# Attention stages of a two-block transformer kernel: row maxima two units ahead, gate passes ahead of the value product

## The chip, the core and the metric

The kernel runs on one core of one Trainium2 chip. The metric is device time in microseconds (us) of one execution. TensorE (PE in the profile; its weight loads are the row PEld) multiplies into PSUM, the banks named `ps`; VectorE is DVE, ScalarE is ACT, GpSimd is POOL, SyncE is SP and issues the DMAs. Each engine has its own instruction stream and works through it in the order written; a stream waits for another engine by semaphores.

## The reference, cut to what matters

Two transformer blocks, each of two layers, work on one sequence of 512 tokens with 1024 channels. The softmax attentions below make up the stages that the change touches. Everything else (projections, convolution, feed-forward) stays as it is.

```python
# first block, per layer: 8 MLA heads (q, k of 96), then 8 heads with two branches each
s = jnp.einsum('bqhd,bkhd->bhqk', qb, k) * scale
p = masked_softmax(s, pos[None, :] <= t[:, None])
o = jnp.einsum('bhqk,bkhd->bqhd', p.astype(dt), v)      # MLA
...
p_s = masked_softmax(s_s, m_s); o_s = einsum(p_s, v_sel)  # selected blocks (at 512 tokens: all blocks)
p_w = masked_softmax(s_w, m_w); o_w = einsum(p_w, v_w)    # window
...
# second block, per layer: 8 sparse heads (a mask of the top 128 keys), 8 forgetting heads
p = jax.nn.softmax(logits, axis=-1); out = jnp.einsum("bqhk,bqkd->bqhd", p, v_sel)
g_a, g_b = jnp.split(jax.nn.sigmoid(gates), 2, axis=-1)   # gate projections h @ w_in of each mixer
```

## The kernel before

The engines' streams are written by hand, one function for each stage. `attention_stage` is one such function and is run six times: in both layers of the first block for the MLA heads (8 units, called latent) and for the two branches (16 units, `nb` is 2), and in both layers of the second block for 8 sparse and 8 forgetting heads (16 units). A unit is one head (of one branch) over all 512 queries. Beside the units the stage computes some tiles of the gate projection ("filler", class `Beside`): 2 tiles in the MLA stage, 5 in the others, three passes of 8 matmuls for each tile, spread over the units by the list `unit_of`. The pass with index n is issued by `passes(u)` where `unit_of[n] == u`; the first pass stands ahead of unit 0 and the last behind the last unit.

The pieces of a unit u, with the letters that the text uses for them:

- S(u), `score`, TensorE line 1190: scores of the four query tiles into three PSUM banks, 8 matmuls in three groups (query tile 3; tiles 0 and 2; tile 1). Each group waits until `exps` of unit u-1 has read that bank.
- M(u), `rowmax`, VectorE line 1246: adds the mask and takes the row maximum, four instructions each followed by a short read of the accumulator, in the same three groups; M0, M1, M2 are the groups.
- E(u), `exps`, ScalarE line 1283: the exponentials, after the maxima of their group.
- X(u), `turn`, TensorE line 1201: ten 128x128 transposes of the probabilities into three other banks. It waits for E(u) and, bank by bank, for L(u-1).
- H(u), ScalarE line 1314: copies the transposed probabilities to SBUF, rounded (the high part).
- L(u), `lows`, VectorE line 1254: three subtractions that make the low part. Each waits for its H.
- V(u), `product`, TensorE line 1213: 8 matmuls, four with the high part (V_hi, after H(u)) and four with the low part (V_lo, after all of L(u)). V also waits for the sum of unit u-1.
- The sum of unit u, `finish`: ScalarE line 1290 copies one half of the result after V(u), VectorE line 1260 adds the other half.
- F, a filler pass, TensorE line 546: 8 matmuls.

What orders the engines before, for the step u of the loop: TensorE issues S(u+1), V(u-1), F if there is one, X(u). VectorE issues M(u+1), the sum of u-1, L(u). ScalarE issues E(u+1), the sum of u-1, H(u), and in some units the copy of a finished gate tile and the rounding of the next weights. The score banks exist once, so S(u+1) follows E(u); the probabilities exist twice.

For 16 units and 5 tiles `unit_of` leaves units 5, 10 and 15 without a filler pass; for 8 units and 2 tiles the passes between first and last stand in units 0, 2, 4 and 6.

Of the kernel before, what the change touches and what calls it, by code (L numbers as in the profile page):

```python
# [41 lines left out]
n = 0  # L42
# [6 lines left out]
n = 0  # L49
# [32 lines left out]
n = 0  # L82
# [113 lines left out]
def take(eng, what):  # L196

    if what:
        eng.wait_ge(*what)
# [910 lines left out]
SCORE_BANKS = ((0, ((3, 0),)), (1, ((0, 0), (2, 128))), (2, ((1, 0),)))  # L1110
# [33 lines left out]
def attention_stage(m, nb, terms, values, masks, causal, out, totals, column, gates=(), base=0, taps=None, late=None, heads=NH, begun=Begun()):  # L1144
# [5 lines left out]
    NU = heads * nb  # L1150
    prob, pt, low, side = m.prob, m.pt_hi, m.pt_lo, m.o_side
    mx = m.small[:, 0:8]
    with stage(m, "masked scores maxed exped transposed hi_out lo_out pv_done side_out o_out multiplied tapped cut " + Beside.NAMES) as (block, (
            masked, scores, maxed, exped, transposed, hi_out, lo_out, pv_done, side_out, o_out, multiplied, tapped, cut, *side_sems)):
        fill = Beside(m, base, gates, 7, side_sems)
        inner = 3 * len(gates) - 2
        unit_of = [-1] + [n * NU // inner for n in range(inner)] + [NU]

        @block.sync
        def _(sp):  # L1160
            for u in range(NU):
                if u % 3 == 1:
                    fill.load(sp, u // 3)

        def rows(j):
            return slice(64 * (j % 2), 64 * (j % 2) + 64)
# [4 lines left out]
        @block.tensor  # L1171
        def _(pe):
            def score(u):
                j, b = divmod(u, nb)
                if late and u == late[0]:
                    pe.wait_ge(cut, late[1])
                if u == NH:
                    for ready in begun.late_operands:
                        pe.wait_ge(*ready)
                for g, (bank, parts) in enumerate(SCORE_BANKS):  # L1180
                    if u:
                        pe.wait_ge(exped, 3 * (u - 1) + g + 1)
                    elif begun.banks:
                        pe.wait_ge(*begun.banks(bank))
                    for qt, c in parts:
                        w = P * (qt + 1)
                        o = m.ps[:, bank, c:c + w]
                        products = terms(j, b)
                        for n_, (q, k) in enumerate(products):
                            mm = nc.tensor.matmul(o, q[:, qt * P:(qt + 1) * P], k[:, 0:w], start=(n_ == 0), stop=(n_ == len(products) - 1))  # L1190
                    mm.then_inc(scores, 1)

            def turn(u):
                pe.wait_ge(exped, 3 * u + 3)
                for g, (bank, parts) in enumerate(PT_BANKS):
                    if u:
                        pe.wait_ge(lo_out, 3 * u - 2 + g)
                    for kt, c in parts:
                        for qt in range(kt, TT):
                            at = PROB_AT[qt] + kt * P  # L1200
                            mm = nc.tensor.transpose(m.ps[:, bank, c + (qt - kt) * P:c + (qt - kt + 1) * P], prob[:, u % 2, at:at + P], m.ident)
                    mm.then_inc(transposed, 1)

            def product(u):
                j, b = divmod(u, nb)
                if u:
                    pe.wait_ge(o_out, u)
                elif begun.out_bank:
                    pe.wait_ge(*begun.out_bank)
                for p, (part, ready) in enumerate(((pt, hi_out), (low, lo_out))):  # L1210
                    pe.wait_ge(ready, 3 * u + 3)
                    for kt in range(TT):
                        mm = nc.tensor.matmul(m.ps[:, 6, kt * P:T], values(j, b, kt),  # L1213
                                              m.r(part)[:, PT_AT[kt]:PT_AT[kt] + T - kt * P],
                                              start=(p == 0 and kt == 0), stop=(p == 1 and kt == TT - 1))
                mm.then_inc(pv_done, 1)

            def passes(u):
                for n in range(inner + 2):
                    if unit_of[n] == u:  # L1220
                        fill.product(pe, n)

            fill.begin(pe)
            take(pe, begun.side_bank)
            passes(-1)
            for ready in begun.operands:
                pe.wait_ge(*ready)
            score(0)
            for u in range(NU):
                if u + 1 < NU:  # L1230
                    score(u + 1)
                if u:
                    product(u - 1)
                passes(u)
                turn(u)
            passes(NU)
            product(NU - 1)

        @block.vector
        def _(dve):  # L1240
            def rowmax(u):
                for g, (bank, parts) in enumerate(SCORE_BANKS):
                    dve.wait_ge(scores, 3 * u + g + 1)
                    for qt, c in parts:
                        s = m.ps[:, bank, c:c + P * (qt + 1)]
                        r = nc.vector.tensor_tensor_reduce(s, s, masks(u // nb, qt), -1.0, HUGE, ALU.add, ALU.min,  # L1246
                                                           mx[:, 4 * (u % 2) + qt:4 * (u % 2) + qt + 1])
                    r.then_inc(maxed, 1)

            def lows(u):  # L1250
                for g, (bank, parts) in enumerate(PT_BANKS):
                    at, w = PT_SPAN[bank]
                    dve.wait_ge(hi_out, 3 * u + g + 1)
                    nc.vector.tensor_tensor(m.r(low)[:, at:at + w], m.ps[:, bank, 0:w], m.r(pt)[:, at:at + w].bitcast(F32), ALU.subtract)\  # L1254
                        .then_inc(lo_out, 1)

            def finish(u):
                j, b = divmod(u, nb)
                dve.wait_ge(side_out, u + 1)
                nc.vector.tensor_tensor(out(b, j // 2)[rows(j), :], m.ps[rows(j), 6, :], side[rows(j), :], ALU.add).then_inc(o_out, 1)  # L1260

            dve.wait_ge(masked, 2)
            take(dve, begun.masks)
            rowmax(0)
            for u in range(NU):
                if u + 1 < NU:
                    rowmax(u + 1)
                if u:
                    finish(u - 1)
                lows(u)  # L1270
            finish(NU - 1)

# [1451 lines left out]
def first_layer(m, begun):  # L2724
# [10 lines left out]
    normed = head_norm_stage(m, gates[0:3], begun)  # L2735
    after = lambda tile: lambda j, qt: tile[:, T - P * (qt + 1):T]
    latent = attention_stage(m, 1, lambda j, b: ((m.q_mla[0:MQK, j, :], m.k_mla[0:MQK, j, :]),), lambda j, b, kt: m.r(m.v_mla)[:, kt, j, :],
                    after(m.causal_wide), m.causal_wide, lambda b, pair: m.o_mla[:, pair, :], m.totals, lambda j, b: 2 * NH + j, gates=gates[3:5], base=C1["gate"] + 3,
                    taps=TAPS_FRONT, begun=normed)
    compressed = compressed_attention_stage(m, gates[5:9], C1["gate"] + 5, latent)  # L2740


    add_x = lambda bank, n: nc.vector.tensor_tensor(m.x[:, n, :], m.x[:, n, :], bank, ALU.add)
    attended = attention_stage(
        m, 2, lambda j, b: [(m.r(m.q_cut)[:, j, :], m.r(k)[:, 2 * b + j // 4, :]) for k in (m.k_hi, m.k_lo)],
        lambda j, b, kt: m.r(m.v_nsa)[:, kt, 2 * b + j // 4, :], after(m.causal_wide), m.causal_wide,
# [595 lines left out]
def second_layer(m, front):  # L3342
# [29 lines left out]
    def wout_modulations(dve, g, mod_added):  # L3372
# [3 lines left out]
    passed, begun = front  # L3376
    recycle(m, passed.passed, 1)
    attended = attention_stage(
        m, 1, terms, lambda j, b, kt: m.r(m.va)[:, kt, :] if j < NH else m.r(m.v_fox)[:, kt, j - NH, :],
        lambda j, qt: m.select_bf[qt] if j < NH else m.tiles_at(1)[:, T - P * (qt + 1):T], m.tiles_at(1),  # L3380
# [406 lines left out]
```

## Time and profile before

| | |
|---|---|
| median of 3 runs | 3469.65 us (3469.04 to 3473.26) |
| profiled execution, its own time | 3466.5 us |
| its span in the profile | 3464.7 us |
| busy share of the span | PE 98%, PEld 80%, DVE 58%, POOL 46%, ACT 41% |
| chain that ended last | PE 81%, DVE 8%, ACT 6%, issue 3%, POOL 1% |
| granted TensorE clock, mean | 0.99 |

Busy shares are means over the whole program. Counted from the first S to the last V, the attention stages of one layer each take 49.58 us (MLA), 95.77 us (branches) and 98.15 us (second block); with two layers of both blocks that is some 487 us of the span. The profiled execution's time is the span and the little that lies around it.

### The profile page before, as it was taken

The page shows a single profiled execution, that of the slowest core. Times are in us where ns is not written, and L with a number is a line of the kernel's source. Part 1 is how long each engine was busy: PE and PEld are TensorE (multiplying, and loading weights), DVE is VectorE, ACT ScalarE, POOL GpSimd, SP SyncE. Part 2 cuts the span into 40 slices and gives each one's busy share as a digit, 9 for nine tenths or more (in the row PEclk, how much of TensorE's full clock was granted, in tenths as well). Part 3 has the DMA queues.
Part 4 walks back from the last instruction along what each step waited for, and adds up shares of the span by engine and source line. Part 5 has one row for each costly group of instructions (what it writes and reads, how often), then busy time and mean ns, then how long its engine had stood idle before and what let it go on. Part 6 is the DMA issues. An engine that isn't in the chain of part 4 may idle for free.

```text
span 3464.7 us, 44113 instructions
## 1 busy us (share of the span) xinstructions
PE 3383.9 (98%) x15780; PEld 2783.4 (80%) x15780; DVE 2022.3 (58%) x3204; ACT 1437.8 (41%) x2513; POOL 1578.3 (46%) x825
## 2 busy tenths in 40 slices
PE   9999999999999999999999999999999999999998
PEld 7877787888888777878888877888888877788887
DVE  6775766112367756751224666769965666758963
ACT  3256743332333567342323447333333447333332
POOL 3357454444434573544443641435543641435543
PEclk9999999999999999999999999999999999999999
DMA  4311123222332111322343221532343221532323
GB/s 172 109 56 43 37 90 111 97 97 97 114 107 98 43 45 44 119 92 97 115 145 111 68 92 55 176 122 107 129 146 129 68 92 50 179 116 105 133 94 101
DMA packets 96890, 346.65 MB, mean 100 GB/s; under 512 B 12640, under 2 KB 13408, under 8 KB 96096
## 3 DMA queue, kind: packets, MB, share of 16 engines
q1 hardware_dynamic: 96736, 344.62, 29.0%
q8 instruction: 94, 1.54, 0.2%
q14 instruction: 60, 0.49, 0.0%
HBM read 338.15 MB, written 6.29 MB: 99 GB/s over the span
## 4 chain that ended last, share of the span: by engine, by line
PE 81%; DVE 8%; ACT 6%; issue 3%; POOL 1%; DMA 0%; ACTq 0%; DVEq 0%; SPq 0%; POOLq 0%
PE ps L391 41%; PE ps L800 16%; PE ps L1410 4%; PE ps L546 4%; ACT arena L1283 3%; PE ps L402 3%; DVE split L1254 3%; PE ps L1690 2%; PE ps L458 1%; PE ps L786 1%; DVE ps L1246 1%; PE ps L1900 1%; PE ps L1190 1%; DVE arena L1260 1%; ACT arena L1290 1%
## 5 line engine op out<-in xcount | busy, mean ns | idle before, releaser
L314 POOL TENSOR_TENSOR weights_lo<-arena,weights_hi 128x1024 fp32r<-128x1024 f32 x466 | 1178.2, 2529 | 1514.5 <-ACT weights_hi L285 1374.7
L285 ACT ACTIVATE weights_hi<-arena 128x1024 fp32r<-128x1024 f32 x490 | 516.7, 1055 | 624.6 <-PE ps L800 377.3
L391 PE MATMUL ps<-moving_hi,weights_hi 128*128 128x512 f32 x2176 | 545.3, 393 | 3.3 <-ACTq L278 1.9
L391 PE MATMUL ps<-moving_lo,weights_hi 128*128 128x512 f32 x2176 | 538.0, 389 | 0.0
L391 PE MATMUL ps<-moving_hi,weights_lo 128*128 128x512 f32 x2176 | 537.9, 389 | 0.0
L391 PEld LDWEIGHTS ps<-moving_hi,weights_hi 128*128 128x128 f32 x2176 | 405.7, 188 | 91.7 <-ACT weights_hi L285 4.0
L391 PEld LDWEIGHTS ps<-moving_hi,weights_lo 128*128 128x128 f32 x2176 | 408.3, 188 | 84.0
L391 PEld LDWEIGHTS ps<-moving_lo,weights_hi 128*128 128x128 f32 x2176 | 407.4, 188 | 84.2
L335 DVE TENSOR_TENSOR moving_lo<-arena,moving_hi 128x512 fp32r<-128x512 f32 x196 | 207.6, 1109 | 224.5 <-ACT moving_hi L330 224.4
L2706 DVE SCALAR_TENSOR_TENSOR arena<-ps,arena 128x512 f32 x64 | 44.1, 692 | 294.5 <-PE ps L391 272.6
L1283 ACT ACTIVATE arena<-ps,arena 128x512 f32<-128x512 f32 (+1 forms) x320 | 166.2, 526 | 119.4 <-DVE arena L1246 119.2
L530 POOL TENSOR_TENSOR weights_lo<-arena,weights_hi 128x512 fp32r<-128x512 f32 x72 | 94.7, 1325 | 244.1 <-ACT weights_hi L285 146.6
L800 PE MATMUL ps<-moving_lo,weights_hi 128*128 128x512 f32 x800 | 197.8, 389 | 1.4 <-DVE moving_lo L335 1.4
L800 PE MATMUL ps<-moving_hi,weights_lo 128*128 128x512 f32 x800 | 197.6, 389 | 0.0
L800 PE MATMUL ps<-moving_hi,weights_hi 128*128 128x512 f32 x800 | 197.6, 389 | 0.0
L1246 DVE CUSTOM_DVE_ANT_0 ps<-ps,arena 128x512 f32<-128x512 f32 (+1 forms) x320 | 147.4, 521 | 58.1 <-PE ps L1190 58.1
L3221 ACT ACTIVATE arena<-ps 128x512 f32<-128x512 f32 x88 | 52.5, 599 | 300.9 <-PE ps L391 298.3
L800 PEld LDWEIGHTS ps<-moving_lo,weights_hi 128*128 128x128 f32 x800 | 150.0, 188 | 33.3 <-DVE moving_lo L335 2.3
L800 PEld LDWEIGHTS ps<-moving_hi,weights_lo 128*128 128x128 f32 x800 | 150.2, 188 | 31.2
L800 PEld LDWEIGHTS ps<-moving_hi,weights_hi 128*128 128x128 f32 x800 | 150.2, 188 | 31.1
L1213 PE MATMUL ps<-split,split 128*128 128x512 f32 (+3 forms) x640 | 129.7, 332 | 21.4 <-ACT split L1314 19.5
L3279 DVE SCALAR_TENSOR_TENSOR arena<-arena 128x512 f32<-128x512 f32 x88 | 144.7, 1682 | 0.0
(390 smaller groups left out, 5313.8 us busy)
## 6 DMA issues: line engine op xcount, KB each, us to landing
arena<-wstream SPq DMA_DIRECT2D x532, 512.0 KB, 3.3
arena<-modw SPq DMA_DIRECT2D x64, 512.0 KB, 3.8
arena<-modw_first SPq DMA_DIRECT2D x32, 512.0 KB, 4.1
layer_input<-arena SPq DMA_DIRECT2D x2, 2048.0 KB, 10.3
arena<-layer_input SPq DMA_DIRECT2D x2, 2048.0 KB, 8.2
arena<-xT SPq DMA_DIRECT2D x4, 512.0 KB, 5.2
outT<-arena SPq DMA_DIRECT2D x8, 256.0 KB, 2.1
arena<-con SPq DMA_DIRECT2D x1, 1285.0 KB, 9.9
```

The lines of the kernel that those rows point to most:

```text
L285: m.nc.scalar.activation(m.w_hi[:, j % 2, :], slab(m, base + at), ACT.Copy).then_inc(hi_ready, 1)
L314: m.nc.gpsimd.tensor_tensor(m.w_lo[:, j % 2, :], slab(m, base + (j if at is None else at)), m.w_hi[:, j % 2, :].bitcast(F32), ALU.subtract)\
L335: return m.nc.vector.tensor_tensor(m.a_lo[:, k, :], tile, m.a_hi[:, k, :].bitcast(F32), ALU.subtract)
L391: mm = m.nc.tensor.matmul(bank, unit_tile(w, k), a[:, k, :], start=(p == 0 and k == 0), stop=(p == 2 and k == KD - 1))
L402: return m.nc.tensor.matmul(banks[c], unit_tile(w[:, c, :], k), a[:, k, :], start=start, stop=stop)
L546: mm = m.nc.tensor.matmul(self.bank(j), unit_tile(w[:, j % 2, :], k), a[:, k, :], start=(p == 0 and k == 0), stop=(p == 2 and k == KD - 1))
L800: mm = nc.tensor.matmul(m.ps[:, 4 * half + n, :], unit_tile(w[:, j % 2, :], 2 * n + k), a[:, 2 * h + k, :], start=(first and p == 0 and k ...
L1213: mm = nc.tensor.matmul(m.ps[:, 6, kt * P:T], values(j, b, kt), m.r(part)[:, PT_AT[kt]:PT_AT[kt] + T - kt * P], start=(p == 0 and kt == 0) ...
L1246: r = nc.vector.tensor_tensor_reduce(s, s, masks(u // nb, qt), -1.0, HUGE, ALU.add, ALU.min, mx[:, 4 * (u % 2) + qt:4 * (u % 2) + qt + 1])
L1283: a = nc.scalar.activation(prob[:, u % 2, PROB_AT[qt]:PROB_AT[qt] + P * (qt + 1)], m.ps[:, bank, c:c + P * (qt + 1)], ACT.Exp, bias=mx[:, ...
L1410: mm = nc.tensor.matmul(m.ps[:, 2 * j + n, :], unit_tile(w[:, j % 2, :], 4 * n + k), a[:, 4 * (b % 2) + k, :], start=(p == 0 and k == 0), ...
L3279: nc.vector.scalar_tensor_tensor(acc[:, s, :], u[:, s, 0:T], column(cw, f), acc[:, s, :], ALU.mult, ALU.add).then_inc(tap3, 1)
```

## The change

It edits three places of `attention_stage`. VectorE takes the maxima of units 0 and 1 ahead of the loop, and in step u those of unit u+2: groups 0 and 1, then the sum of u-1, then group 2, then L(u). TensorE issues the filler pass of a unit ahead of V instead of behind it, and the pass of unit 0 between S(0) and S(1). `unit_of` is stretched so that its last inner pass falls in the last unit: for 16 units the units without a pass are 4, 9 and 14; for 8 units the passes stand in units 0, 2, 4 and 7. No instruction is added or taken away; ScalarE, GpSimd and SyncE keep their streams but for the units in which gate tiles are copied out.

```diff
@@ -1154,7 +1154,7 @@
             masked, scores, maxed, exped, transposed, hi_out, lo_out, pv_done, side_out, o_out, multiplied, tapped, cut, *side_sems)):
         fill = Beside(m, base, gates, 7, side_sems)
         inner = 3 * len(gates) - 2
-        unit_of = [-1] + [n * NU // inner for n in range(inner)] + [NU]
+        unit_of = [-1] + [n * (NU - 1) // (inner - 1) for n in range(inner)] + [NU]
 
         @block.sync
         def _(sp):
@@ -1226,20 +1226,22 @@
             for ready in begun.operands:
                 pe.wait_ge(*ready)
             score(0)
+            passes(0)
             for u in range(NU):
                 if u + 1 < NU:
                     score(u + 1)
                 if u:
+                    passes(u)
                     product(u - 1)
-                passes(u)
                 turn(u)
             passes(NU)
             product(NU - 1)
 
         @block.vector
         def _(dve):
-            def rowmax(u):
-                for g, (bank, parts) in enumerate(SCORE_BANKS):
+            def rowmax(u, groups):
+                for g in groups if u < NU else ():
+                    bank, parts = SCORE_BANKS[g]
                     dve.wait_ge(scores, 3 * u + g + 1)
                     for qt, c in parts:
                         s = m.ps[:, bank, c:c + P * (qt + 1)]
@@ -1261,12 +1263,13 @@
 
             dve.wait_ge(masked, 2)
             take(dve, begun.masks)
-            rowmax(0)
+            rowmax(0, (0, 1, 2))
+            rowmax(1, (0, 1, 2))
             for u in range(NU):
-                if u + 1 < NU:
-                    rowmax(u + 1)
+                rowmax(u + 2, (0, 1))
                 if u:
                     finish(u - 1)
+                rowmax(u + 2, (2,))
                 lows(u)
             finish(NU - 1)
```

VectorE, the MLA stage, one step of its loop before (`scores_1_4` counts groups of S, `side_out_1_4` the halves that ScalarE copied, `hi_out_1_4` the copies H; 128x512, 128x128, 128x384 and 128x256 are query tiles 3, 0, 2 and 1):

```order
L1246 ISA ps,arena<-ps,arena 128x512 [waits scores_1_4]
L1246 ISA arena 128x1
L1246 ISA ps,arena<-ps,arena 128x128 [waits scores_1_4]
L1246 ISA arena 128x1
L1246 ISA ps,arena<-ps,arena 128x384
L1246 ISA arena 128x1
L1246 ISA ps,arena<-ps,arena 128x256 [waits scores_1_4]
L1246 ISA arena 128x1
L1260 TENSOR_TENSOR arena<-ps,arena 64x512 [waits side_out_1_4]
L1254 TENSOR_TENSOR split_55<-ps,split_55 128x512 [waits hi_out_1_4] x2
L1254 TENSOR_TENSOR split_55<-ps,split_55 128x256 [waits hi_out_1_4]
```

The same step of the changed program (its line numbers are two higher):

```order
L1248 ISA ps,arena<-ps,arena 128x512 [waits scores_1_4]
L1248 ISA arena 128x1
L1248 ISA ps,arena<-ps,arena 128x128 [waits scores_1_4]
L1248 ISA arena 128x1
L1248 ISA ps,arena<-ps,arena 128x384
L1248 ISA arena 128x1
L1262 TENSOR_TENSOR arena<-ps,arena 64x512 [waits side_out_1_4]
L1248 ISA ps,arena<-ps,arena 128x256 [waits scores_1_4]
L1248 ISA arena 128x1
L1256 TENSOR_TENSOR split_55<-ps,split_55 128x512 [waits hi_out_1_4] x2
L1256 TENSOR_TENSOR split_55<-ps,split_55 128x256 [waits hi_out_1_4]
```

The sum (64x512) now stands between the third and the fourth maximum. The difference that the rows' names don't show is the unit: the maxima before are those of unit u+1 and now those of unit u+2, while the three subtractions behind them are those of unit u in both.

TensorE, the MLA stage, from the end of S(3) to the start of X(2), before:

```order
L1190 MATMUL ps<-arena 128x256 [waits exped_1_4]
L1213 MATMUL ps<-split_55,split_53 128x512 [waits hi_out_1_4,o_out_1_4]
L1213 MATMUL ps<-split_55,split_53 128x384
L1213 MATMUL ps<-split_55,split_53 128x256
L1213 MATMUL ps<-split_55,split_53 128x128
L1213 MATMUL ps<-split_55,split_53 128x512 [waits lo_out_1_4]
L1213 MATMUL ps<-split_55,split_53 128x384
L1213 MATMUL ps<-split_55,split_53 128x256
L1213 MATMUL ps<-split_55,split_53 128x128
L546 MATMUL ps<-moving_hi,weights_lo 128x512 [waits fill_lo_1_4]
L546 MATMUL ps<-moving_hi,weights_lo 128x512 x7
L1201 MATMUL ps<-arena 128x128 [waits lo_out_1_4,exped_1_4]
```

The same place in the changed program:

```order
L1190 MATMUL ps<-arena 128x256 [waits exped_1_4]
L546 MATMUL ps<-moving_hi,weights_lo 128x512 [waits fill_lo_1_4]
L546 MATMUL ps<-moving_hi,weights_lo 128x512 x7
L1213 MATMUL ps<-split_55,split_53 128x512 [waits hi_out_1_4,o_out_1_4]
L1213 MATMUL ps<-split_55,split_53 128x384
L1213 MATMUL ps<-split_55,split_53 128x256
L1213 MATMUL ps<-split_55,split_53 128x128
L1213 MATMUL ps<-split_55,split_53 128x512 [waits lo_out_1_4]
L1213 MATMUL ps<-split_55,split_53 128x384
L1213 MATMUL ps<-split_55,split_53 128x256
L1213 MATMUL ps<-split_55,split_53 128x128
L1201 MATMUL ps<-arena 128x128 [waits lo_out_1_4,exped_1_4]
```

The filler pass (`L546`) stands ahead of the value product of unit 1 (`L1213`, its second half waits for `lo_out_1_4`, the subtractions) and X (`L1201`) directly behind it. S stays where it was: behind X of the unit before, ahead of both.

## Rows read from the trace of the kernel before

The columns of a window are: stretch in us from the start of the span and its length, busy us (and number of instructions) of PE, PEld, DVE, ACT and POOL, the granted clock of TensorE (1.00 is 2.4 GHz), the busy share of the DMA engines, GB/s. A row of a timeline is: start in us, length in us from the first start to the last end, engine, line, operation, what it writes and reads, shape, how many instructions are merged in the row, and in brackets the idle time ahead of it with what ended it.

**Rows 1.** Windows of three attention stages, first S to last V.

```profile
234.46:284.04 49.58, 46.30 (x241) 35.01 (x240) 32.32 (x95) 33.98 (x97) 32.19 (x33) 1.00 0.06 22
321.82:417.59 95.77, 89.48 (x521) 76.30 (x520) 64.84 (x191) 71.31 (x199) 51.80 (x48) 1.00 0.09 28
2047.87:2146.02 98.15, 93.88 (x522) 76.75 (x520) 65.11 (x191) 71.32 (x199) 10.85 (x9) 1.00 0.09 28
```

**Rows 2.** Timeline of TensorE, selected and window branches, one unit and one wait.

```profile
341.07 1.51 PE L1190 MATMUL ps<-split,split 128*128 128x512 f32 x8
342.50 1.66 PE L1213 MATMUL ps<-split,split 128*128 128x512 f32 x8
344.00 2.06 PE L546 MATMUL ps<-moving_lo,weights_hi 128*128 128x512 f32 x8
345.90 1.25 PE L1201 MATMUL ps<-arena 128*128 128x128 f32 x10
346.91 1.51 PE L1190 MATMUL ps<-split,split 128*128 128x512 f32 x8
...
360.21 1.66 PE L1213 MATMUL ps<-split,split 128*128 128x512 f32 x8 [1.48 <-ACT split L1314]
```

**Rows 3.** Timeline of TensorE, MLA heads, a unit without filler.

```profile
254.58 2.32 PE L1190 MATMUL ps<-arena 96*128 96x512 f32 x8
256.56 1.57 PE L1213 MATMUL ps<-split,split 128*128 128x512 f32 x8
257.96 1.27 PE L1201 MATMUL ps<-arena 128*128 128x128 f32 x10
259.07 2.32 PE L1190 MATMUL ps<-arena 96*128 96x512 f32 x8
```

**Rows 4.** Timeline of TensorE, forgetting heads of the second block, one S.

```profile
2090.76 2.32 PE L1190 MATMUL ps<-arena 66*128 66x512 f32 x8
```

**Rows 5.** The waits of all engines, one line: us in total, times, longest.

```profile
DVE arena L1260 <- ACT arena L1290: 144.0, 80, 2.3
```

**Rows 6.** Timeline of TensorE and of VectorE, first unit of the branches.

```profile
321.82 1.43 PE L1190 MATMUL ps<-split,split 128*128 128x512 f32 x8
...
322.58 0.70 DVE L1246 CUSTOM_DVE_ANT_0 ps<-ps,arena 128x512 f32<-128x512 f32 x1 [7.81 <-PE ps L1190]
```

**Rows 7.** Timeline of VectorE, selected and window branches, one unit.

```profile
346.84 0.69 DVE L1260 TENSOR_TENSOR arena<-ps,arena 64x512 f32<-64x512 f32 x1 [1.77 <-ACT arena L1290]
347.56 1.62 DVE L1254 TENSOR_TENSOR split<-ps,split 128x512 fp32r<-128x512 f32 x3
349.10 0.69 DVE L1246 CUSTOM_DVE_ANT_0 ps<-ps,arena 128x512 f32<-128x512 f32 x1
...
350.47 0.47 DVE L1246 CUSTOM_DVE_ANT_0 ps<-ps,arena 128x256 f32<-128x256 f32 x1
...
350.85 0.14 DVE L1246 DVE_READ_ACCUMULATOR2_ANT arena<- 128x1 f32 x1
```

**Rows 8.** Timeline of TensorE and its weight loads, second half of one V.

```profile
349.24 0.71 PEld L1213 LDWEIGHTS ps<-split,split 128*128 128x128 f32 x4 [0.23 <-DVE split L1254]
...
349.93 2.07 PE L546 MATMUL ps<-moving_hi,weights_lo 128*128 128x512 f32 x8
```

**Rows 9.** Timeline of TensorE and of VectorE, first unit of the MLA heads.

```profile
234.46 2.32 PE L1190 MATMUL ps<-arena 96*128 96x512 f32 x8
...
235.64 0.70 DVE L1246 CUSTOM_DVE_ANT_0 ps<-ps,arena 128x512 f32<-128x512 f32 x1 [2.39 <-PE ps L1190]
236.39 0.30 DVE L1246 CUSTOM_DVE_ANT_0 ps<-ps,arena 128x128 f32<-128x128 f32 x1
```

**Rows 10.** Timeline of TensorE, first filler after the MLA heads.

```profile
287.85 2.10 PE L546 MATMUL ps<-moving_hi,weights_hi 128*128 128x512 f32 x8 [2.43 <-ACTq L278]
```

**Rows 11.** Windows around that row, and early in the program.

```profile
284.00:290.00 6.00, 3.57 (x20) 2.97 (x18) 1.21 (x3) 4.38 (x8) 2.14 (x2) 1.00 0.02 4
18.00:20.40 2.40, 2.40 (x7) 1.92 (x6) 2.40 (x4) 1.16 (x2) 1.79 (x1) 0.50 1.00 430
```

## The prediction

> **What bounds it now.** I read the windows of the attention stages first, then TensorE's timeline inside them, then VectorE's, then the waits. In the windows TensorE's busy time is 46.30 of 49.58 us, 89.48 of 95.77 and 93.88 of 98.15, at a granted clock of 1.00; VectorE and ScalarE are busy for two thirds to three quarters [rows 1]. So TensorE bounds the stages, and what can be won is the few per cent in which it waits. A unit of the branches that has a filler pass is, by starts of TensorE's rows, S 1.43 us, V 1.50, F 1.90 and X 1.01, 5.84 in all, with no wait in it [rows 2]. A unit without filler has 3.94 us of such work, less than what the other engines need for a unit, and there V waits, 1.48 us in the case shown, for the copies H [rows 2]. For the MLA heads S takes 1.98, V 1.40 and X 1.11, 4.49 without and 6.39 with filler [rows 3]; the forgetting heads' S has the same 2.32 us row [rows 4], so I take the MLA numbers for them. VectorE's largest wait in these stages is the sum of a unit waiting for ScalarE's half, 144.0 us over 80 units [rows 5], beside TensorE's work and not on the path.
>
> **What the change makes of the order.** Before, L(u) follows M(u+1), whose scores were made a whole unit ahead of V(u). Now L(u) is queued on VectorE behind M(u+2), so it waits for S(u+2). TensorE issues S(u+2), F, V(u), X(u+1), S(u+3) in that order, and V_lo(u) needs L(u). This closes a ring that a unit cannot be shorter than: S(u+2) starts; M(u+2), the sum and L(u) run on VectorE; V_lo(u); X(u+1); S(u+3) starts. While V_lo waits, X(u+1) and S(u+3) are queued behind it on TensorE, and ScalarE's next work waits for these; while M(u+2) waits, the sum and L(u) are queued behind it on VectorE. Nothing on VectorE can run between the end of L(u) and the first group of S(u+3).
>
> **The length of the ring.** From the start of S to the start of M0: 0.76 us, seen where VectorE stood idle [rows 6]. From M0 to M2: 1.37; M2 until the next instruction may start, at the read of its accumulator: 0.38; L with its three parts to its end: 1.62 [rows 7]. The sum: its row has 0.69, and L's end overlaps the next start by 0.08 (347.56 + 1.62 against 349.10), so 0.61 [rows 7]. L ends at 349.18 and the weights of V_lo load from 349.24: 0.06; from there to the start of what follows: 0.69 [rows 7, 8]. X: 1.01 [rows 2]. Sum: 0.76 + 1.37 + 0.61 + 0.38 + 1.62 + 0.06 + 0.69 + 1.01 = 6.50 us, against 5.84 of TensorE's own work. For MLA and forgetting heads S to M0 is 1.18 (234.46 to 235.64), the next maximum then starts 0.75 later instead of M0's 0.69 less 0.08, so 0.14 more [rows 7, 9], and X is 1.11 [rows 3]: 7.16 us against 6.39. Whether a unit has a filler no longer matters, since 1.43 + 1.90 + 0.75 (V_hi, half of V) = 4.08 us end before L does, at 0.76 + 1.37 + 0.61 + 0.38 + 1.62 = 4.74.
>
> What I could not read is a sum directly behind a maximum, since it always waited. Below: each of the joints M1 to sum, sum to M2 and M2 to L overlaps by 0.08 more, 0.24 off, ring 6.26. Above: the accumulator reads (0.14 each, after M1 and M2 [rows 7]) don't overlap with what follows and the sum takes its 0.69, 0.36 on, ring 6.86. I take 6.50, since in VectorE's rows a read starts together with the instruction that follows it.
>
> **The sums by stage**, from the first S to the last V, p for TensorE's step in which S(p+1) is issued.
> - Start, common to all: S, F, S, X. Branches 1.43 + 1.90 + 1.43 + 1.01 = 5.77; MLA 1.98 + 1.90 + 1.98 + 1.11 = 6.97. The filler of unit 0 now covers the first wait for exponentials; this gain is in the sum.
> - Step p = 1 has no sum of an earlier unit: ring less 0.61, 5.89 or 6.55.
> - End, with no S left: F, V, X, F, 1.90 + 1.50 + 1.01 + 1.90 = 6.31. H and L run under F, so the wait of the last units goes; this gain too is in the sum.
> - Branches: 5.77 + 5.89 + 13 x 6.50 + 6.31 = 102.5, before 95.77 [rows 1]: +6.7.
> - MLA: 6.97 + 6.55 + 5 x 7.16 + 6.31 = 55.6, before 49.58: +6.1.
> - Second block (five steps with sparse scores, eight with forgetting ones): 5.77 + 5.89 + 5 x 6.50 + 8 x 7.16 + 6.31 = 107.8, before 98.15: +9.6.
>
> Two layers each: 2 x 22.4 = +44.7 us, over 68 rings (2 x (14 + 6 + 14)). The profiled execution took 3466.5 us, so 3511.2; it lies 3.15 us under the median of the runs, 3469.65, so a median of **3514 us**.
>
> Costed at nothing: the filler pass ahead of V by itself (its 1.90 us lie under the 4.74 us of VectorE's chain; without that cover V would start 1.90 us later and nothing would be lost, as X follows directly); the longer list `unit_of` (the same passes); GpSimd's low halves of weights and SP's loads, which wait for passes that now come in longer steps; VectorE's wait for the sum, 144.0 us, off the path before and gone now, since ScalarE's half is ready a step earlier.
>
> TensorE will stand idle for about 0.7 us in a unit with filler and 6.50 - 3.94 = 2.6 us in one without. Ahead of the first filler behind the MLA heads it idled for 2.43 us, and the granted clock of that window is 1.00, the 2.4 GHz level [rows 10, 11], so I price no clock. The Trainium skill, TensorE: Matmul & The Clock Gate, Part 1, says that an idle TensorE is put back to 1.2 GHz until it has been busy again; no such fall is in these rows. By the rows the sum stays; by that rule it would grow as in the third rival.
>
> **Rivals.**
> 1. *It does what its pieces suggest: TensorE waits no more.* For it: every wait named in the stages ends with H, L or the sum, and fillers cover the start and the end. Against: L(u) is behind M(u+2). It needs the ring to be under TensorE's own work in units with filler, 5.84 and 6.39. All waits gone would leave 88.1 (5.77 + 11 x 5.84 + 3 x 3.94 + 6.31) for the branches, 44.0 for MLA (6.97 + 2 x 6.39 + 4 x 4.49 + 6.31) and 92.5 for the second block (steps 1 to 6 five with filler, 7 to 14 six), 18.8 us a layer pair, 2 x 18.8 = 37.6: 3432 us. This is the other side: the change wins from the point where the mean ring is shorter than mine by more than 44.7/68 = 0.66 us.
> 2. *The ring is near that point.* It would take joints on VectorE, the wake-ups and V_lo that together are 0.56 to 0.76 us shorter than rows 6 to 9 make them: within 7 us of 3470. Each piece is a row, which leaves little room.
> 3. *The clock falls.* With an idle stretch in every unit, TensorE might be granted 0.50, the 1.2 GHz level, as early in the program [rows 11]. Its part of a ring, 0.76 + 0.69 + 1.01 = 2.46 us, would at most double: 68 x 2.46 = 167 us on top, up to 3681. Against it stand rows 10 and 11.
> 4. *The ring closes but is shorter*, at the lower bounds of its joints or somewhat below: 68 x 0.24 = 16 us less, 3498, down to 3480.
>
> **Numbers.** The forecast with its upper bound, 3505 to 3539 (68 x 0.36 = 24 us up): 0.75. Rival 4: 0.11. Rival 3: 0.04. Rival 2: 0.04. Rival 1: 0.06. A measurement of this kernel can tell about 0.2%, 7 us, from no change: faster 0.06, same 0.04, slower 0.90. Range 3490 to 3545, which takes in the bounds and the upper part of rival 4.
>
> **What the changed profile would show.** The distance from S to S in the branches is 6.5 us in units with and without filler alike, 7.2 in the MLA and forgetting heads. V_lo's weight loads wait for L in nearly every unit, where before V's waits named H and the sum; M0 waits for S in every unit, by 0.06 + 0.69 + 1.01 + 0.76 = 2.5 us; the sum waits for nothing; the waits at the start and the end of each stage are gone. TensorE's busy share of the branches' window falls towards 88/102. The prediction is wrong if S to S stays at 5.84 us in units with filler, which would mean that L(u) ends before TensorE reaches V_lo, or if the granted clock in these windows is under 1.00.

## The result and the profile after

| | before | after |
|---|---|---|
| median | 3469.35 us (3468.32 to 3473.26, 4 runs) | 3547.68 us (3543.84 to 3548.54, 4 runs) |
| span of the profiled execution | 3464.7 us | 3545.0 us |
| granted TensorE clock, mean | 0.99 | 0.982 |

The changed kernel is slower by a ratio of 1.0222 (95% interval 1.0204 to 1.0239): +78 us where +44.7 was forecast, and 3 us above the stated range of 3490 to 3545. The direction and the ring held; two terms that lengthen it were missing from the sum, the joints of odd heads and the clock.

Windows of the three attention stages of the kernel after, first S to last V, columns as in [rows 1]:

```profile
236.38:295.56 59.18, 49.43 (x241) 38.40 (x240) 32.82 (x95) 34.70 (x97) 32.13 (x33) 0.94 0.05 18
336.05:442.73 106.68, 90.03 (x521) 78.53 (x520) 64.87 (x191) 71.50 (x199) 51.84 (x48) 0.97 0.08 26
2101.47:2213.77 112.30, 97.08 (x521) 79.99 (x520) 65.81 (x191) 72.21 (x199) 10.81 (x9) 0.97 0.07 24
```

The forecast was 55.6, 102.5 and 107.8. Over all six stages (the second layers have 57.60, 109.81 and 114.08) the sum is 559.65 against 487.00 before, +72.65 of the 80.3 us by which the span grew. The clock is no longer 1.00, which the prediction had named as a sign that it is wrong.

Waits of all engines after (us in total, times, longest), the rows that concern the units:

```profile
DVE ps L1248 <- PE ps L1190: 249.0, 86, 16.3
...
PEld ps L1213 <- DVE split L1256: 63.8, 68, 1.4
...
DVE arena L1262 <- ACT arena L1293: 37.5, 18, 2.8
...
PEld ps L1213 <- DVE arena L1262: 29.0, 18, 1.7
```

The largest wait of [rows 5], the sum waiting for ScalarE's half, has shrunk from 144.0 to 37.5 us; the forecast had it gone, but it is left 18 times. In its place VectorE waits for S 86 times, where the same view of the kernel before has

```profile
DVE ps L1246 <- PE ps L1190: 58.1, 18, 16.0
```

V_lo's weights wait for L 68 times: as often as there are rings in the forecast, 6 in each MLA stage and 14 in each of the others. The last row of the four is V_hi, which in units without a pass waits for the sum. Taking away a large wait that was off the path has put a new one on it.

Timeline of TensorE after, branches, a unit without a pass and two with one:

```profile
360.72 1.52 PE L1190 MATMUL ps<-split,split 128*128 128x512 f32 x8
363.76 0.85 PE L1213 MATMUL ps<-split,split 128*128 128x512 f32 x4 [1.52 <-DVE arena L1262]
365.86 0.85 PE L1213 MATMUL ps<-split,split 128*128 128x512 f32 x4 [1.25 <-DVE split L1256]
366.55 1.27 PE L1201 MATMUL ps<-arena 128*128 128x128 f32 x10
367.58 1.51 PE L1190 MATMUL ps<-split,split 128*128 128x512 f32 x8
368.93 2.02 PE L546 MATMUL ps<-moving_hi,weights_lo 128*128 128x512 f32 x8
...
374.45 1.51 PE L1190 MATMUL ps<-split,split 128*128 128x512 f32 x8
...
380.89 1.52 PE L1190 MATMUL ps<-split,split 128*128 128x512 f32 x8
```

From S to S it is 6.86 without a pass, 6.87 with one, and 6.44 with one in the next unit. So a pass makes no difference, as forecast; something else does. Timeline of VectorE after, the same stretch: first the long unit, then the short one.

```profile
368.32 0.70 DVE L1248 CUSTOM_DVE_ANT_0 ps<-ps,arena 128x512 f32<-128x512 f32 x1 [2.52 <-PE ps L1190]
...
369.19 0.60 DVE L1248 CUSTOM_DVE_ANT_0 ps<-ps,arena 128x384 f32<-128x384 f32 x1
...
369.88 0.69 DVE L1262 TENSOR_TENSOR arena<-ps,arena 64x512 f32<-64x512 f32 x1
370.60 0.43 DVE L1248 CUSTOM_DVE_ANT_0 ps<-ps,arena 128x256 f32<-128x256 f32 x1
...
371.06 1.61 DVE L1256 TENSOR_TENSOR split<-ps,split 128x512 fp32r<-128x512 f32 x3
...
376.06 0.60 DVE L1248 CUSTOM_DVE_ANT_0 ps<-ps,arena 128x384 f32<-128x384 f32 x1
...
376.57 0.68 DVE L1262 TENSOR_TENSOR arena<-ps,arena 64x512 f32<-64x512 f32 x1
377.18 0.41 DVE L1248 CUSTOM_DVE_ANT_0 ps<-ps,arena 128x256 f32<-128x256 f32 x1
...
377.51 1.61 DVE L1256 TENSOR_TENSOR split<-ps,split 128x512 fp32r<-128x512 f32 x3
```

The first sum is one of an odd head, whose half of the result lies on partitions 64 to 127; the second is one of an even head, on partitions 0 to 63. From the last maximum of group 1 to the sum, from the sum to M2 and from M2 to L it is 0.69, 0.72 and 0.46 for the odd head, 0.51, 0.61 and 0.33 for the even one: 1.87 against 1.45, each from start to start. An odd head's ring is 0.42 us longer.

The second loss is the clock. Timeline of TensorE after, another unit without a pass of the same stage, and the windows of its parts:

```profile
397.26 0.85 PE L1213 MATMUL ps<-split,split 128*128 128x512 f32 x4 [1.52 <-DVE arena L1262]
399.36 1.43 PE L1213 MATMUL ps<-split,split 128*128 128x512 f32 x4 [1.25 <-DVE split L1256]
400.59 2.35 PE L1201 MATMUL ps<-arena 128*128 128x128 f32 x10
402.60 2.69 PE L1190 MATMUL ps<-split,split 128*128 128x512 f32 x8
```

```profile
381.75:394.18 12.43, 10.44 (x64) 9.19 (x63) 8.09 (x24) 7.52 (x24) 6.07 (x6) 1.00 0.11 42
...
399.40:401.00 1.60, 1.60 (x6) 1.50 (x7) 0.00 (x0) 0.17 (x1) 1.49 (x2) 0.50 0.00 0
401.00:405.00 4.00, 4.00 (x18) 3.81 (x17) 0.85 (x3) 2.21 (x5) 3.85 (x4) 0.50 0.14 22
```

The two waits are those of the unit at 363.76, but now X takes 2.35 us instead of 1.27 and S 2.69 instead of 1.52, at 0.50, the 1.2 GHz level; this interval from S to S is 8.39 us. Each of the six stages has one to three such places. Behind the MLA heads it happens too. Timeline of TensorE after, the row that answers to [rows 10], and the window of that row:

```profile
299.37 3.51 PE L546 MATMUL ps<-moving_hi,weights_hi 128*128 128x512 f32 x8 [2.43 <-ACTq L278]
```

```profile
299.30:303.00 3.70, 3.63 (x11) 2.93 (x11) 0.00 (x0) 3.58 (x7) 3.46 (x3) 0.55 0.02 7
```

The idle time ahead of it is 2.43 us as before, but the row takes 3.51 instead of 2.10 us, at a mean clock of 0.55. From the last V of the MLA heads to the first S of the branches it is 40.49 us (before 37.78: +2.7; in the second layer +2.8).

### The profile page after: what moved, and what is told of

It reads as the page before. It is cut to its first block, busy times and chain, and to the rows that moved or that the text cites. A ratio compares the mean times of both kernels' runs of the same rounds, so it can differ in the third digit from the quotient of the medians.

```text
span 3545.0 us, 44113 instructions
## 1 busy us (share of the span) xinstructions
PE 3406.6 (96%) x15780; PEld 2804.8 (79%) x15780; DVE 2031.7 (57%) x3204; ACT 1441.7 (41%) x2513; POOL 1582.1 (45%) x825
## 4 chain that ended last, share of the span: by engine, by line
PE 84%; DVE 11%; issue 2%; ACT 1%; POOL 1%; SPq 1%; DMA 0%; DVEq 0%; ACTq 0%; POOLq 0%
PE ps L391 40%; PE ps L800 15%; PE ps L1413 4%; PE ps L546 3%; DVE split L1256 3%; PE ps L402 3%; DVE ps L1248 3%; PE ps L1201 3%; PE ps L1190 3%; PE ps L1213 2%; PE ps L1693 2%; PE ps L458 1%; PE ps L786 1%; DVE arena L1262 1%; PE ps L1903 1%
## 5 line engine op out<-in xcount | busy, mean ns | idle before, releaser
L1213 PE MATMUL ps<-split,split 128*128 128x512 f32 (+3 forms) x640 | 132.3, 333 | 79.2 <-DVE split L1256 53.4
L1213 PEld LDWEIGHTS ps<-split,split 128*128 128x128 f32 x640 | 112.8, 194 | 108.4 <-DVE split L1256 63.8
```

## The experiments

Times are medians against runs of the kernel before on the same chip (medians 3469.7 to 3472.4). The theory: the ring through VectorE (S, M, sum, M2, L, V_lo, X, S) sets the step. The rival at the start: the place of the pass, or the list, costs the time. After the first results: what, beside the ring, makes up the missing 33 us.

**1. VectorE's order put back, the rest changed.**

```diff
-            rowmax(1, (0, 1, 2))
             for u in range(NU):
-                rowmax(u + 2, (0, 1))
+                rowmax(u + 1, (0, 1, 2))
                 if u:
                     finish(u - 1)
-                rowmax(u + 2, (2,))
                 lows(u)
```

> Only VectorE's order is put back (M(u+1), sum, L(u)); the filler pass ahead of V, the early pass of unit 0 and the stretched list stay. Ring theory (L(u) queued behind M(u+2) closes a ring of 6.4 to 7.5 us): S to S returns to 5.84 us in branch units with filler, the stretches at the low clock go, and the waits at the start and end of the stages stay away: about 2 x 6 = 12 us under the kernel before, 3455 to 3466 us. Rival (the filler's new place or the new list costs the time): still above 3520 us.

Measured 3476.99 us, ratio 1.002 (1.0011 to 1.0028). The ring is gone: steps of the branches with a pass take 5.44 to 5.94 us where the wait told below is not (the stage's first takes 6.27). So the rival falls: with the other edits in place nearly the whole loss goes. But the pieces gain nothing either, and the time is 11 us above the forecast. Timeline of TensorE in this run, first stage of the branches:

```profile
338.60 3.09 PE L546 MATMUL ps<-moving_hi,weights_hi 128*128 128x512 f32 x8 [1.97 <-ACT arena L557]
```

A pass ahead of V comes at once behind S and waits for the copy-out of the tile before it (L557, 12 times, 20.7 us), V behind it; in 4 of the 12 it then runs at the lower clock, as here. The prediction costed this edit at nothing; under the ring that is right, without it the pass has this wait of its own.

**2. Only VectorE's maxima ahead**, TensorE's order (below) and the list as before.

```diff
             score(0)
-            passes(0)
             for u in range(NU):
                 if u + 1 < NU:
                     score(u + 1)
                 if u:
-                    passes(u)
                     product(u - 1)
+                passes(u)
                 turn(u)
```

> Only the maxima two units ahead; TensorE's order and the list are those of before, so F stands between V and X. Ring theory: F now lies inside the ring, 1.90 us more in each unit with filler, 12 + 3 + 12 such steps in the three stages of a layer pair: 2 x 27 x 1.90 = 103 us on top of the changed kernel, 3635 to 3660 us, S to S in branch units with filler 8.3 to 8.8 us. Rival (TensorE's new order costs the time): between 3469 and 3500 us.

Measured 3716.48 us, ratio 1.0713 (1.0698 to 1.0729), slower still than the theory's 3635 to 3660. Timeline of TensorE in this run, branches:

```profile
374.24 0.85 PE L1213 MATMUL ps<-split,split 128*128 128x512 f32 x4 [1.53 <-DVE arena L1261]
376.34 1.06 PE L1213 MATMUL ps<-split,split 128*128 128x512 f32 x4 [1.25 <-DVE split L1255]
377.20 3.46 PE L546 MATMUL ps<-moving_hi,weights_lo 128*128 128x512 f32 x8
```

The pass is now part of the ring, between V_lo and X, and it runs at the lower level: 3.46 us instead of the 2.06 of [rows 2]. The stages' clock is 0.83 to 0.88 but for the first (0.97). So moving the pass ahead of V is what keeps the ring from costing three times as much, and the clock falls with the maxima ahead as the only edit.

**3. The sum ahead of the maxima**, all else changed.

```diff
-                rowmax(u + 2, (0, 1))
                 if u:
                     finish(u - 1)
-                rowmax(u + 2, (2,))
+                rowmax(u + 2, (0, 1, 2))
                 lows(u)
```

> The changed kernel, with the sum of u-1 ahead of all maxima of u+2, where VectorE waits for S(u+2) anyway. Ring theory: the ring loses the sum (0.61 us, and 0.42 more in odd heads): 5.84 us in the branches (TensorE's own work), 6.45 in the MLA and forgetting heads; 2 us over the kernel before from the sum over the stages, and up to 15 more if the clock still falls in units without filler: 3471 to 3487 us. Rival (the sum is hidden and the time is the clock's): about 3547 us.

Measured 3502.3 us, ratio 1.0093 (1.008 to 1.0106). Clean steps are 5.89 to 6.05 and 6.51 as the ring without the sum gives them, odd and even heads alike; but others of 7.0 to 10.7 stand between them and the stages' clock is 0.94 to 0.98. The ring's length is confirmed by its parts; the time is 15 us above the forecast, and run 6 shows that this is the clock.

**4. The sum of odd heads started at partition 0**, over 128 partitions, so that it overwrites the even head's half of the output. `upto(j)` is `slice(0, 64 * (j % 2) + 64)`.

```diff
-                nc.vector.tensor_tensor(out(b, j // 2)[rows(j), :], m.ps[rows(j), 6, :], side[rows(j), :], ALU.add).then_inc(o_out, 1)
+                nc.vector.tensor_tensor(out(b, j // 2)[upto(j), :], m.ps[upto(j), 6, :], side[upto(j), :], ALU.add).then_inc(o_out, 1)
```

> The changed kernel, but the sum of an odd head is taken over all 128 partitions from partition 0 instead of over partitions 64 to 127; what is added into the even head's half is left wrong. Theory (the joints around a sum that starts at partition 64 don't overlap, 0.42 us): rings of 6.87 and 7.48 become 6.45 and 7.06, 28 rings x 0.42 = 12 us less, 3533 to 3540 us. Rival (the long rings have another cause, as GpSimd's or ScalarE's work in those units): 3547 us and the same two lengths.

Measured 3538.37 us, ratio 1.0206 (1.0189 to 1.0224). Timeline of VectorE in this run, an odd head's sum (now 128x512) and what follows:

```profile
362.94 0.60 DVE L1251 CUSTOM_DVE_ANT_0 ps<-ps,arena 128x384 f32<-128x384 f32 x1
...
363.46 0.69 DVE L1265 TENSOR_TENSOR arena<-ps,arena 128x512 f32<-128x512 f32 x1
364.06 0.42 DVE L1251 CUSTOM_DVE_ANT_0 ps<-ps,arena 128x256 f32<-128x256 f32 x1
...
364.40 1.62 DVE L1259 TENSOR_TENSOR split<-ps,split 128x512 fp32r<-128x512 f32 x3
```

With twice the partitions the instruction takes the same 0.69, and the joints are 0.52, 0.60 and 0.34, the even head's. From the second ring of a stage on, every clean step is 6.44 to 6.46 or 7.05 to 7.07 (6.52 where sparse heads give way to forgetting ones). The MLA stages, both at a clock of 1.00, take 55.13 us (forecast 55.6); a branches stage at 0.98 takes 103.10 (102.5). Where neither missing term acts, the forecast's sum holds.

**5. The idle time filled:** two spare matmuls of 256 columns into V's bank ahead of V, in the units without a pass.

```diff
+                if u + 1 < NU and u + 1 not in unit_of:
+                    keep_busy(m, 6, 2)
                 for p, (part, ready) in enumerate(((pt, hi_out), (low, lo_out))):
```

> The changed kernel; in a unit without filler TensorE runs two spare 256-column matmuls into V's bank ahead of V, where it stood idle. Clock theory (some 20 us of the slowdown are stretches at 0.50 of the clock that start in units without filler): the rings of 8.0 to 9.0 us become 6.45 to 7.5, the granted clock of the stages 0.99 to 1.00, 3520 to 3532 us. Rival (the long rings in these units are waits of another engine): 3540 us or more and the same rings.

Measured 3520.54 us, ratio 1.0146 (1.013 to 1.0161). Windows of its first three stages:

```profile
234.76:290.74 55.98, 49.70 (x257) 38.28 (x256) 32.81 (x95) 34.47 (x97) 32.10 (x33) 1.00 0.05 19
328.50:432.72 104.22, 89.80 (x534) 78.22 (x532) 64.70 (x191) 71.26 (x199) 51.71 (x48) 1.00 0.08 26
...
2078.57:2188.94 110.37, 97.83 (x534) 80.39 (x532) 65.68 (x191) 71.94 (x199) 10.81 (x9) 0.98 0.08 25
```

From the second ring of a stage on, the steps are 6.44 to 6.46, 6.86 to 6.88, 7.05 to 7.07 and 7.47 to 7.49 (6.52 where the kind of head changes), with a single 8.37. Work that computes nothing makes the changed kernel 27 us faster, since TensorE keeps its clock: the clean steps have not moved. What is left, +51, is the ring: 44.7 forecast, plus 28 odd rings by 0.42, less 4 for a ring slightly shorter than forecast, makes 52.

**6. Both: the sum first and the idle time filled** (the edits of 3 and 5).

> The changed kernel with the sum ahead of the next unit's maxima on VectorE (as in the run with the sum first) and two spare matmuls of 256 columns ahead of the value product in the units without a pass. Theory (what is left of that run's +32.6 over before is TensorE's clock): units of 5.9 to 6.05 and 6.5 as there, no interval above 7 in the stages of branches, granted clock of the stages 0.98 to 1.00, stages of about 52.5 (MLA), 95 to 97 (branches) and 100 to 102 (second block), and a time of 3472 to 3484. Rival (the excess is a wait of the order itself): intervals of 7.5 and more stay and the time stays at 3495 or above.

Measured 3477.94 us, ratio 1.0022 (1.0013 to 1.0031). Windows of its first three stages:

```profile
234.98:287.35 52.37, 48.89 (x257) 38.56 (x256) 32.88 (x95) 34.17 (x97) 32.14 (x33) 1.00 0.06 21
325.13:420.33 95.20, 88.40 (x534) 77.98 (x532) 64.79 (x191) 70.74 (x199) 51.81 (x48) 1.00 0.09 29
2056.43:2156.26 99.83, 95.11 (x534) 79.27 (x532) 65.68 (x191) 71.19 (x199) 10.84 (x9) 1.00 0.08 27
```

No step is longer than 6.52, the clock is 1.00. The branches are 0.57 us shorter than in [rows 1], MLA 2.8 and the second block 1.7 longer, where a ring of 6.51 stands against a mean of 5.9 (a unit with and one without a pass) and 6.38. The six stages take 494.8 us, +7.8 over before: the whole difference.

**7. The changed kernel with the list of before**, units 5, 10 and 15 (MLA: 1, 3, 5 and 7) without a pass.

```diff
-        unit_of = [-1] + [n * (NU - 1) // (inner - 1) for n in range(inner)] + [NU]
+        unit_of = [-1] + [n * NU // inner for n in range(inner)] + [NU]
```

> The changed kernel with the list of passes of before: units without a pass are 5, 10 and 15, and 1, 3, 5 and 7 of the MLA heads. The ring doesn't depend on passes, so clean units stay 6.45 / 6.87 and 7.06 / 7.48. Theory (the ring's two waits in a unit without a pass, 1.5 and 1.25, bring the clock down wherever the unit stands; the list costs little): one or two intervals of 7.8 to 9 in each stage, granted clock of the stages 0.94 to 0.98, 3535 to 3552. Rival (the list is what brings the clock down, as it did by itself in the kernel before): stages clean at a clock of 0.99 to 1.00, 56 to 57, 103 to 105 and 109 to 111 long, and a time of 3515 to 3527.

Measured 3538.96 us, ratio 1.0194 (1.0181 to 1.0208); the stages' clock is 0.91 to 0.97, with steps of 8.2 to 10.5, a little beyond the forecast of both. The theory holds: the ring's waits bring the clock down with either list.

**8. The kernel before with the stretched list alone** (the edit of 7 the other way round, in the kernel before).

> The kernel before with the stretched list of passes alone: VectorE's order and the place of a pass (behind the value product) are as before. Theory: the wait of the units without a pass (about 1.48 each) moves from the end of a stage to three units spread in it and the two or three units at the end have none, so that a stage changes by less than 1 and the time lies within 5 of before, 3465 to 3475. Rival (a lone unit without a pass costs the clock): granted clock of the stages below 0.98 and a time above 3478.

Measured 3493.78 us, ratio 1.0062 (1.0048 to 1.0075): the theory falls and the rival holds. Timeline of TensorE in this run, branches, the unit that answers to the wait in [rows 2]:

```profile
359.36 2.33 PE L1213 MATMUL ps<-split,split 128*128 128x512 f32 x8 [1.48 <-ACT split L1314]
361.50 3.09 PE L546 MATMUL ps<-moving_hi,weights_lo 128*128 128x512 f32 x8
```

The same wait of 1.48 us that V has before is here followed by the lower level (stage clock 0.95): V takes 2.33 instead of the 1.66 it has there, and the pass 3.09 instead of 2.06. It isn't always so even within this run. The same unit of the second block's stage, in its first and in its second layer:

```profile
2101.77 1.75 PE L1213 MATMUL ps<-split,split 128*128 128x512 f32 x8 [1.47 <-ACT split L1314]
...
2888.34 2.08 PE L1213 MATMUL ps<-split,split 128*128 128x512 f32 x8 [1.48 <-ACT split L1314]
```

The pass behind the first takes 2.07 us, the one behind the second 3.33, at 0.50.

**9. The same with the spare matmuls of 5.**

> The kernel before with the stretched list and two spare matmuls of 256 columns ahead of the value product of the units without a pass (the spare ones run in the wait of about 1.48). Theory (the stretched list cost its 23 us in the run without spare matmuls through TensorE's clock alone): granted clock of the stages 0.99 to 1.00, no interval above 8 behind a stage's first, stages of 49.5 to 50.5, 95.5 to 97 and 98 to 99.5, and a time of 3464 to 3477. Rival (the list costs by a wait of its own): intervals of 9 and a time of 3485 or above.

Measured 3482.94 us, ratio 1.0037 (1.0025 to 1.0049): between the two. About half of the list's 23 us goes with the idle time filled, so that much was the clock in its units without a pass; the MLA stages are still at 0.97. At a clock of 1.00 a branches stage still takes 97.62, 1.85 more than before. Timeline of TensorE in this run, end of that stage:

```profile
417.95 1.65 PE L1215 MATMUL ps<-split,split 128*128 128x512 f32 x8 [2.55 <-ACT split L1316]
```

Before, the row at the same place (413.13) waited 1.19. With unit 14 left without a pass, and V(14) ahead of the last unit's pass, nothing covers H there. So the list has a wait of its own in the order of before; in the changed kernel the pass stands ahead of V and covers it.

**10. VectorE's order and the pass behind V as before, the pass of unit 0 between S(0) and S(1), the stretched list.** Of the edit against the kernel before, TensorE's part:

```diff
             score(0)
+            passes(0)
             for u in range(NU):
                 ...
                 if u:
                     product(u - 1)
+                    passes(u)
-                passes(u)
```

> VectorE's order and the place of F behind V are those of before; only the pass of unit 0 stands between S(0) and S(1), and the list reaches the last unit. Theory: a tile's first pass no longer meets the bank that ScalarE has not copied yet (20.7 us of waits with F ahead of V), and the waits at start and end of a stage (1.2 and 0.9 to 1.2 us, MLA 0.5 and 1.2) go: 12 us under the kernel before, 3455 to 3462 us. Rival (these waits come back inside the stage, as ScalarE is the next bound): 3466 to 3473 us.

Measured 3493.48 us, ratio 1.0067 (1.0054 to 1.0081), a miss. Timeline of TensorE in this run, start of the branches:

```profile
335.59 2.24 PE L1213 MATMUL ps<-split,split 128*128 128x512 f32 x8 [1.67 <-ACT split L1315]
337.63 2.89 PE L546 MATMUL ps<-moving_hi,weights_lo 128*128 128x512 f32 x8
```

The pass covers the first exponentials, and the wait comes back at V(0), 0.31 us before and 1.67 here: the pass that stood between S(1) and X(0) is gone from there. The lower clock stands behind it.

**11. As 1, but of each tile's passes the first stays behind V,** so that it doesn't wait for the copy-out (`passes(u, (1, 2))` ahead of `product(u - 1)`, `passes(u, (0,))` behind it).

> As the last one, but the second and third pass of a tile go ahead of V and only its first pass stays behind V. Theory: V's small waits for H and L are covered too, 3452 to 3460 us. Rival (F ahead of V delays X and with it H, E and the next S): not under the last kernel, or slower than before.

Measured 3472.61 us, ratio 1.0009 (1.0000 to 1.0018): the same as before, a miss. The waits have moved from the copy-out to H (V's waits for it: 31 times, 29.3 us, against 19 times, 13.6 us in run 1). No version tried beats the kernel before.

## Why the prediction was right in direction and too small

- **The ring exists and has the forecast length in even heads.** 6.44 to 6.46 measured against 6.50, 7.06 against 7.16; in odd heads 6.87 and 7.48; alike with and without a pass; M0 waits for S by 2.52 us (2.5 forecast); V_lo's weights wait 68 times. Runs 1 and 3 to 6 take it apart: without the maxima ahead it is gone, and with the sum moved out it is shorter by the sum and its joints.
- **Start and end.** S(0) to S(3) takes 11.78 us in the branches, the forecast's start and step 1 are 5.77 + 5.89 = 11.66. That they agree is partly luck: S(0) to S(2) takes 5.40 and the next step 6.38, since S(2) itself waits for exponentials. The waits at the stages' ends are gone.
- **The step that failed first: "The length of the ring".** The sum's joint was taken as one number for all heads, with an upper bound of 0.36 us. Half the heads lie on partitions 64 to 127 and there the joint costs 0.42 more, in 28 of the 68 rings: 11.8 us. Run 4 shows that it is the start partition. That the odd ring of 6.87 meets the stated upper bound of 6.86 is chance: the bound let the accumulator reads stand free in every head. The rows could have told: the 1.62 us of L overlap the next start by 0.08 in [rows 7], while the sum there, 0.69 long, is followed only 0.72 later. The Trainium skill, VectorE: DVE Perf Modes, section "Two Vector instructions with no wait between them", gives the rule, as a model: an instruction whose inputs or output start in another group of 32 partitions than the last ones read or written in the same memory is held until all earlier ones have finished. The trace agrees: the odd head's sum starts 0.69 behind the start of a maximum of 0.60, and M2 0.72 behind that of a sum of 0.69, where the even head's start 0.51 and 0.61 behind theirs.
- **The step that failed second: "I price no clock".** It rested on one idle stretch of 2.43 us at a clock of 1.00 [rows 10, 11]. After the change the same 2.43 us are followed by 0.55, and in the units without a pass waits of 1.52 and 1.25 by 0.50. Rival 3 named the mechanism, at a chance of 0.04, and bounded it by 167 us; it took about 27 (run 5 against the changed kernel). The Trainium skill, TensorE: Matmul & The Clock Gate, Part 1, also tells of a kernel in which short, frequent idle pieces make the clock swing between its two levels; the traces here agree with that, by the 0.50 behind waits of 1.52 and 1.25.
- **The sum again**, for the stages: 44.7, less 68 x 0.06 for the slightly shorter ring, plus 11.8 for odd heads, plus some 20 by which steps at the lower clock exceed clean ones: some 72, measured 72.65. Of the 7.7 us outside the stages, 5.5 lie behind the MLA heads, at the lower clock; 2.2 I have not assigned.
- **What was costed at nothing** held for the changed kernel's clean steps (run 7 has the same ones with the old list; its time is some 10 us less, which I put down to the clock without having shown it), but not for each edit by itself: ahead of V a pass can wait for the copy-out (run 1), and the list costs 23 us in the order of before (run 8).

What stays open: why the same wait is followed by the lower clock in one program and not in another (1.48 us in [rows 2] and in run 8), and even in one layer and not in the other of one program (run 8). At the end of run 9's stage a wait of 2.55 left the clock at 1.00. The runs show that it depends on more than the length of the wait.

## What to carry to other kernels

When an instruction is queued behind one that works further ahead, follow the chain of waits round through all engines until it comes back to its start: its length, not the total of any wait, is the new step. Read each joint of such a ring for every kind of operand that passes it, above all for each start partition. Where TensorE is near its full clock with some idle time left, price a change that adds waits at both clock levels, and try spare matmuls in the wait: if the time falls, it was the clock.

## What the runs showed of the hardware that was not expected

- A 64x512 sum on partitions 64 to 127 between instructions that start at partition 0 costs VectorE 0.42 us more over its three joints than one on partitions 0 to 63; the same sum over all 128 partitions costs no more than the latter (joints 0.52, 0.60, 0.34).
- The granted clock fell to 0.50 behind waits of 1.25 to 1.5 us, two in a step, and behind a single one of 1.48 (run 8), while a lone wait of 2.43 us in the kernel before left it at 1.00 and the same one after the change did not. Two spare matmuls of 256 columns in each unit without a pass kept it at 1.00 in four of the six stages and were worth 27 us of 3548.
